# First expert layer's weights in 4 MiB transfers with 32 KiB pieces, in a hybrid mixer and mixture-of-experts block

## The chip, the cores and the metric

The kernel runs on one core of a Trainium2 chip. The metric is the device time of one execution in microseconds, from inputs in HBM to output in HBM. It is written in Bass: each engine (TensorE, here PE; VectorE, DVE; ScalarE, ACT; SyncE, SP) has its own instruction stream, and the streams meet only at semaphores. All large loads are DMAs that SP issues, in the order of its program, onto 16 DMA engines.

## The reference

`x` is 256 tokens of width 1024 in float32. A first part mixes tokens in three branches (an RWKV-7 recurrence, sliding-window attention, attention to a memory), gates and merges them, and adds the result to `x`. The second part is where the change lies: a router picks 4 of 32 experts per token, and each expert is a two-layer network.

```python
logits = (xt @ w_router + b_router)
top_vals, top_idx = lax.top_k(logits, TOP_K)
gates = jax.nn.softmax(top_vals, axis=-1)
...
h = x_pad[tok] @ w1[e] + b1[e]              # w1[e]: 1024 x 2048, 8 MiB
y = clamped_swiglu(h) @ w2[e] + b2[e]       # w2[e]: 1024 x 1024, 4 MiB
...
return rms_norm(h, final_norm_w)
```

The experts' weights are 32 x 12 MiB = 384 MiB, and each is read once.

## The kernel before

**The mixer** runs first. Its weights come in 42 loads (`NMIX`), chunks of at most 1 MiB, in an order that `mixer_chunks` writes out by hand: input projections, memory projections, then for each branch four gate chunks and two branch chunks, and last four chunks of `w_out`.

**The ring.** Weights live in a ring of 16 slots of 1 MiB (`RING`, 8 KiB in each of the 128 partitions). Slots 0 to 5 are narrow ones of their own, at the head of the tensor `ring`. Slots 6 to 15 lie in memory that the mixer uses for other things, at the offsets of `WIDE_AT` (in KiB per partition; offsets below 48 continue the tensor `ring`, the others are in the tensor `upper`). Only the last ten mixer chunks use them, and SP waits before the first load into each region: on `pv_sb`, `y_ps` and `y_rwkv_sb` (lines 366 to 371), which say that what the region held is dead. After the mixer, the experts' weights go round all 16 slots.

**The expert stage.** Each expert takes 12 places of the ring (`CPE`): 8 for the first layer, 4 for the second. `place` turns a running number into a slot. SP's order is: first layer of expert 0, then for each expert r the first layer of r+1 and the second layer of r; at the very end the second layer of the last expert. `load_w1` issues four transfers of 2 MiB per expert, each into two neighbouring slots (`twin_slot`); a partition p gets rows 4p+j and 4p+j+1 of a block of 512 rows, which is 16 KiB in one piece. `load_w2` issues two of 2 MiB, with 16 KiB pieces too, and for the last expert four of 1 MiB.

PE counts each 1 MiB chunk it has used in one semaphore, `slots_used`; before a transfer SP waits until the chunks that were in its slots have been counted. Each transfer announces its landing in `slot_full` of its first slot. PE's order for a pair of experts is in `pair`: `up` of the even expert (first layer, 8 chunks), `down` of the expert before (second layer, 4 chunks), transposes of the activations (`turn`), `up` of the odd expert with the gate transposes and two scatters of the previous pair between its chunks (`between`), `gather` of the next pair's tokens, `down` of the even expert, `turn`. DVE and ACT compute the activation between an `up` and its `turn`. All matrix products go through one helper, so that they carry line 457 in the profile.

After the last pair: `turn_gates`, `down` of the last expert, two scatters, the final norm and the store.

Of the kernel before, what the change touches and what calls it, by code (L numbers as in the profile page):

```python
# [16 lines left out]
P = 128  # L17
D = 1024
T = 256
KC = D // P  # L20
# [10 lines left out]
NCH = T // CH  # L31
# [19 lines left out]
RING = 16  # L51
NARROW = 6
SLOT = 2048
CPE = 12
GROUP = 4
TURNS = GROUP * CPE // RING

WIDE_AT = (88, 96, 72, 80, 0, 8, 16, 24, 32, 40)


PCOLS = {}
# [78 lines left out]
def build(nc, x, mem, w_in, rwkv_w2, rwkv_a2, rwkv_g2, swa_sinks, w_mem_kv, w_gate, w_branch, w_out,  # L140
          ffn_norm_w, w_router, b_router, w_exp1, b_exp1, w_exp2, b_exp2, final_norm_w, params, consts, out):
    order, slots = mixer_chunks()
    NMIX = len(order)
# [7 lines left out]
    with ExitStack() as ctx:  # L151
# [130 lines left out]
        def slot(s):  # L282
            return ring[:, s * SLOT:(s + 1) * SLOT] if s < NARROW else kb(WIDE_AT[s - NARROW], 8)

        def twin_slot(s):
            return ring[:, s * SLOT:(s + 2) * SLOT] if s < NARROW else kb(WIDE_AT[s - NARROW], 16)


        slot_full = [sem(f"slot_full{s}") for s in range(RING)]
        slots_used = sem("slots_used")  # L290
# [56 lines left out]
        def w2_place(i, g, r, final):  # L347
            return place(g, r * CPE + i + (8 if final else 16))

        def rows(w):  # L350
            return w.rearrange("(c p) f -> p c f", p=P)

        @block.sync
        def _(sp):
            for t in range(TT):
                sp.dma_start(xrows[:, t, :], x[0, t * P:(t + 1) * P, :]).then_inc(x_loaded[t], 16)
            sp.dma_start(prm[:], params).then_inc(prm_loaded, 16)
            sp.dma_start(cst[:, 0:2 * P], consts[:, 0:2 * P]).then_inc(ident_loaded, 16)
            w_in_r = rows(w_in[0])
            kv_r = rows(w_mem_kv[0])  # L360
            out_r = rows(w_out[0])
            for n, (name, c) in enumerate(order):
                s = slots[n]
                if previous[n] is not None:
                    sp.wait_ge(slots_used, previous[n] + 1)
                elif s == NARROW:
                    sp.wait_ge(pv_sb, 4)
                elif s == NARROW + 2:
                    sp.wait_ge(y_ps, NCH)
                elif s == NARROW + 6:  # L370
                    sp.wait_ge(y_rwkv_sb, TT)
                wide = slot(s).rearrange("p (c f) -> p c f", c=2)
                if name == "in_rwkv":
                    dst, src = slot(s)[:, 0:C_RWKV], w_in_r[:, c, 0:C_RWKV]
                elif name == "in_rest":
                    dst, src = slot(s)[:, 0:C_REST], w_in_r[:, c, C_RWKV:C_RWKV + C_REST]
                elif name == "mem_kv":
                    dst, src = wide, kv_r[:, 2 * c:2 * c + 2, :]
                elif name == "gate":
                    dst = slot(s).rearrange("p (c f) -> p c f", c=KC)  # L380
                    src = rows(w_gate[0, c[0]])[:, :, c[1] * 256:(c[1] + 1) * 256]
                elif name == "branch":
                    dst = slot(s).rearrange("p (c f) -> p c f", c=4)
                    src = rows(w_branch[0, c[0]])[:, :, c[1] * 512:(c[1] + 1) * 512]
                else:
                    dst, src = wide, out_r[:, 2 * c:2 * c + 2, :]
                sp.dma_start(dst, src).then_inc(slot_full[s], 16)
                if n == 2:
                    sp.dma_start(memrows, mem[0].rearrange("(t p) d -> p t d", p=P)).then_inc(mem_loaded, 16)
                if n == 3:  # L390

                    sp.dma_start(cst[:, 2 * P:], consts[:, 2 * P:]).then_inc(cst_loaded, 16)
                    sp.dma_start(lora[0:64, :], rwkv_w2[0]).then_inc(lora_loaded, 16)
                    sp.dma_start(lora[64:P, :], rwkv_a2[0]).then_inc(lora_loaded, 16)
                    sp.dma_start(gate2, rwkv_g2[0]).then_inc(lora_loaded, 16)
                    sp.dma_start(sinks[:], swa_sinks.to_broadcast([P, 8])).then_inc(sink_loaded, 16)

            sp.dma_start(b2rows[0:NE, :], b_exp2[0]).then_inc(late_loaded, 16)
            for b in range(2):
                sp.dma_start(wrt[:, 4 * b:4 * b + 4, :], w_router[0, b * 512:(b + 1) * 512, :].rearrange("(p c) e -> p c e", c=4)).then_inc(late_loaded, 16)  # L400
            sp.dma_start(brt[:], b_router.to_broadcast([P, NE])).then_inc(late_loaded, 16)

            def load_w1(q, a, r, zero=False):

                g = q * (NE // GROUP) + a
                for c in range(0, KC, 2):
                    s, _, n = w1_place(c, g, r, zero)
                    sp.wait_ge(slots_used, n + (NMIX - RING + 2))
                    b, j = c // 4, c % 4
                    sp.dma_start(twin_slot(s), w_exp1[0, bass.ds(a * GROUP + r, 1), b * 512:(b + 1) * 512, :]  # L410
                                 .rearrange("a (p c) f -> p a c f", c=4)[:, :, j:j + 2, :].rearrange("p a c f -> p (a c f)"))\
                      .then_inc(slot_full[s], 16)

            def load_w2(q, a, r, final=False):
                g = q * (NE // GROUP) + a
                for i in range(0, 4, 1 if final else 2):
                    s, _, n = w2_place(i, g, r, final)
                    sp.wait_ge(slots_used, n + (NMIX - RING + (1 if final else 2)))
                    b, j = i // 2, 2 * (i % 2)
                    src = w_exp2[0, bass.ds(a * GROUP + r, 1), b * 512:(b + 1) * 512, :].rearrange("a (p c) f -> p a c f", c=4)  # L420
                    if final:
                        sp.dma_start(slot(s), src[:, :, j:j + 2, :].rearrange("p a c f -> p (a c f)")).then_inc(slot_full[s], 16)
                    else:
                        sp.dma_start(twin_slot(s), src.rearrange("p a c f -> p (a c f)")).then_inc(slot_full[s], 16)

            def load_group(q, a, count=GROUP):

                for r in range(count):
                    load_w1(q, a, r + 1)
                    load_w2(q, a, r)  # L430

            def load_pass(q, very_first=False):
                load_w1(q, 0, 0, True)
                if very_first:
                    load_group(q, 0)
                with sp.Fori(1 if very_first else 0, NE // GROUP - 1) as a:
                    load_group(q, a)
                load_group(q, NE // GROUP - 1, GROUP - 1)
                load_w2(q, NE // GROUP - 1, GROUP - 1, True)

                for t in range(TT):
                    sp.wait_ge(final_sb, q * TT + t + 1)
                    sp.dma_start(out[0, t * P:(t + 1) * P, :], outrow[:, t, :]).then_inc(stored, 16)

            load_pass(0, True)
            sp.wait_ge(stored, TT * 16)
            sp.wait_ge(route_done, 1)
            most = sp.value_load(cnti[0:1, 0:1], min_val=0, max_val=T)
            with sp.If(most > SLOTS):
                with sp.Fori(1, PASSES) as q:  # L450
                    load_pass(q)
                sp.wait_ge(stored, PASSES * TT * 16)

        @block.tensor
        def _(pe):
# [439 lines left out]
            def up(g, r, E, N, parity, between, zero=False):  # L895

                for c in range(KC):
                    s, times, n = w1_place(c, g, r, zero)
                    if parity == 0 and c % 4 == 0:
                        pe.wait_ge(xg_sb, N * 2 + c // 4 + 1)  # L900
                    if c % 2 == 0:
                        pe.wait_ge(slot_full[s], times * 16 + 16 * uses[s])
                    for z in range(2):
                        for hf in range(2):
                            last = mm(ps[64 * hf:64 * hf + 64, z, :], xg[:, c, parity * SLOTS:(parity + 1) * SLOTS],
                                      slot(s)[:, hf * D + z:(hf + 1) * D:2], c == 0, c == KC - 1)
                    last.then_inc(slots_used, 1)
                    if between:
                        between(c)
                pe.wait_ge(slots_used, n + (NMIX + 1))  # L910
                pe.sem_inc(up_ps, 1)  # L911

            def down(q, g, r, E, final=False):

                pe.wait_ge(actT_sb, E + 1)
                for i in range(4):
                    s, times, n = w2_place(i, g, r, final)
                    if i % 2 == 0:
                        pe.wait_ge(slot_full[s], times * 16 + 16 * uses[s])
                    elif final:  # L920
                        pe.wait_ge(slot_full[s], q * 16 + 16 * (uses[s] + 1))
                    for cc in range(2):
                        k = 2 * i + cc
                        for dh in range(2):
# [821 lines left out]
```

## Time and profile before

| | us |
|---|---|
| median of 3 runs | 1319.02 (1318.52 to 1319.63) |
| the profiled execution | 1318.95 |
| its span, first to last instruction | 1317.1 |
| PE busy | 1221.2 (93%) |
| DVE busy | 349.0 (27%) |
| ACT busy | 199.0 (15%) |
| bytes moved | 449.72 MB, mean 341 GB/s over the span |

The page divides the span in 40 slices of 32.9 us. The mixer takes the first 11 or so, the experts the rest. A busy digit of PE means that matmuls were in its pipe, not that it ran at its peak. Landing time of a DMA counts from its issue, so it contains the wait behind transfers issued before it.

### The profile page before, as it was taken

To read this page: it belongs to the slowest core of one execution; us is meant where nothing else is said; L and a number is where in the kernel's file an instruction comes from. 1 tells how busy PE (TensorE), PEld (TensorE's weight loads), DVE (VectorE), ACT (ScalarE), POOL (GpSimd) and SP (SyncE) were. 2 spreads that over 40 slices of the span, in tenths; PEclk is the share of its full clock that TensorE was granted. 3 is DMA by queue.
4 is the path that set the end of the run, shared out by engine and by line. 5 is a ranking of instruction groups with operands and counts; after the bars stand their busy time and mean duration, and the time that the engine had idled before them with its cause. 6 is when DMAs were issued, how large, how long until landed. Compare 5 with 4: busy or idle time off the path is not lost.

```text
span 1317.1 us, 15444 instructions
## 1 busy us (share of the span) xinstructions
PE 1221.2 (93%) x6534; PEld 599.7 (46%) x6534; DVE 349.0 (27%) x574; ACT 199.0 (15%) x381; POOL 0.2 (0%) x4
## 2 busy tenths in 40 slices
PE   7999989999989999999999889898989989898986
PEld 6886778888553333333323233232323323232322
DVE  2146472211123221231212222121222222121222
ACT  1224522200121110111101011110101011110102
POOL 0000000000000000000000000000000000000000
PEclk9999999999979999999999999999999999999998
DMA  8353201595449999999999999999999999999994
GB/s 340 114 165 131 65 3 34 196 389 197 145 153 399 426 428 426 428 428 429 427 427 428 429 429 428 426 429 429 428 428 428 427 429 428 429 428 428 426 427 197
DMA packets 50799, 449.72 MB, mean 341 GB/s; under 512 B 4512, under 2 KB 17184, under 8 KB 25920
## 3 DMA queue, kind: packets, MB, share of 16 engines
q1 hardware_dynamic: 50272, 447.48, 82.2%
q10 hardware_dynamic: 480, 1.57, 0.4%
q8 instruction: 34, 0.56, 0.2%
q14 instruction: 13, 0.11, 0.0%
HBM read 447.99 MB, written 1.05 MB: 341 GB/s over the span
## 4 chain that ended last, share of the span: by engine, by line
PE 63%; DMA 30%; DVE 4%; ACT 1%; issue 1%; SPq 0%; PEldq 0%; DVEq 0%
PE ps L457 61%; DMA ring<-in_w_exp 30%; DVE ring L1380 0%; PE ps L934 0%; DVE upper L1471 0%; PE ps L692 0%; DMA xrows<-in_x 0%; ACT ring L1134 0%; PE ps L473 0%; ACT factors L1261 0%; DVE upper L1585 0%; PE ps L601 0%; DVE ring L1377 0%; ACT ring L1160 0%; PE ps L842 0%
## 5 line engine op out<-in xcount | busy, mean ns | idle before, releaser
L457 PE MATMUL ps<-ring,upper 128*64 128x512 f32 (+4 forms) x2928 | 572.0, 535 | 40.8 <-DMA ring<-in_w_exp 36.3
L457 PEld LDWEIGHTS ps<-ring,upper 128*64 128x64 f32 (+2 forms) x2928 | 181.6, 137 | 392.0 <-issue 325.6
L457 PE MATMUL ps<-upper 128*64 128x512 f32 (+6 forms) x1624 | 282.3, 441 | 17.0 <-DMA upper<-in_w_exp 8.2
L457 PEld LDWEIGHTS ps<-upper 128*64 128x64 f32 (+3 forms) x1624 | 143.3, 162 | 147.9 <-issue 129.2
L457 PE MATMUL ps<-xT,ring 128*128 128x256 f32 x672 | 150.7, 382 | 0.0
L457 PEld LDWEIGHTS ps<-xT,ring 128*128 128x128 f32 x672 | 127.2, 191 | 18.6 <-issue 1.3
L1668 DVE TENSOR_TENSOR xrows<-xrows,ps 128x1024 f32<-128x1024 f32 x32 | 39.1, 1221 | 314.2 <-PE ps L457 314.2
L1647 DVE TENSOR_TENSOR upper<-ps,merged 128x512 f32<-128x512 f32 x32 | 22.1, 692 | 377.2 <-PEq L911 377.2
L1255 ACT ACTIVATE upper<-upper 128x512 f32<-128x512 f32 x32 | 20.2, 631 | 544.0 <-DVE upper L1650 544.0
L1261 ACT ACTIVATE factors<-ps 64x512 f32<-64x512 f32 x64 | 37.9, 592 | 202.7 <-PEq L929 201.9
L457 PE MATMUL ps<-factors,upper 128*128 128x512 f32 x128 | 63.2, 617 | 1.5 <-ACT factors L1261 1.5
L457 PE MATMUL ps<-upper,ring 128*128 128x256 f32 (+1 forms) x272 | 57.3, 371 | 0.0
L457 PEld LDWEIGHTS ps<-upper,ring 128*128 128x128 f32 (+1 forms) x272 | 45.8, 194 | 8.7 <-issue 2.8
L1640 DVE STREAM_SHUFFLE merged<-merged 128x1024 f32<-128x1024 f32 x32 | 43.2, 1351 | 0.0
L457 PEld LDWEIGHTS ps<-factors,upper 128*128 128x128 f32 x128 | 21.8, 189 | 43.7 <-issue 43.7
L1660 DVE TENSOR_TENSOR upper<-upper 128x512 f32<-128x512 f32 x32 | 34.0, 1063 | 1.2 <-ACT upper L1255 0.2
L934 PEld LDWEIGHTS ps<-cst,upper 128*128 128x128 f32 x128 | 13.5, 141 | 37.1 <-issue 35.2
L934 PE MATMUL ps<-cst,upper 128*128 128x128 f32 x128 | 20.9, 286 | 9.3 <-PE ps L457 8.0
L457 PE MATMUL ps<-ring,merged 128*128 128x512 f32 x64 | 27.8, 592 | 0.0
L1509 DVE TENSOR_TENSOR upper<-upper,ps 128x512 f32<-128x512 f32 x8 | 5.5, 688 | 72.3 <-PE ps L457 72.3
L1251 ACT ACTIVATE upper<-ps 128x512 f32<-128x512 f32 x32 | 17.4, 596 | 34.8 <-PE ps L457 34.8
L1655 DVE SCALAR_TENSOR_TENSOR upper<-upper 128x512 f32<-128x512 f32 x32 | 22.2, 693 | 1.1
(210 smaller groups left out, 477.8 us busy)
## 6 DMA issues: line engine op xcount, KB each, us to landing
ring<-in_w_exp SPq DMA_DIRECT2D x142, 2048.0 KB, 32.5
upper<-in_w_exp SPq DMA_DIRECT2D x48, 2048.0 KB, 33.6
ring<-in_w_gate SPq DMA_DIRECT2D x9, 1024.0 KB, 5.1
ring<-in_w_in SPq DMA_DIRECT2D x8, 896.0 KB, 10.5
ring<-in_w_in SPq DMA_DIRECT2D x8, 640.0 KB, 3.9
ring<-in_w_branch SPq DMA_DIRECT2D x5, 1024.0 KB, 5.1
ring<-in_w_mem_kv SPq DMA_DIRECT2D x4, 1024.0 KB, 4.9
ring<-in_w_out SPq DMA_DIRECT2D x4, 1024.0 KB, 14.4
```

The source lines that it names most:

```text
L457: return pe.matmul(o, l, r, start=start, stop=stop, skip_group_check=True)
L934: last = pe.transpose(ps[:, 2, m * P:(m + 1) * P], act_[:, m * P:(m + 1) * P], ident)
L1251: act.activation(xg[:, 4 * b:4 * b + 4, :], ps[:, 4 + b, :].rearrange("p (c s) -> p c s", c=4), ACT.Copy).then_inc(xg_sb, 1)
L1255: act.activation(sig, glu, ACT.Sigmoid, scale=ALPHA).then_inc(sig_sb, 1)
L1261: act.activation(yrow[64 * parity:64 * parity + 64, dh * 512:(dh + 1) * 512], ps[64 * dh:64 * dh + 64, 3, :], ACT.Copy).then_inc(yrow_sb, 1)
L1509: link(TTn(gsig[:, m % 2, :], gsig[:, m % 2, :], ps[:, 7, :], ALU.mult))
L1640: dve.stream_shuffle(b1all, b1rows, [e] * NE).then_inc(b1_spread, 1)
L1647: TTn(glu, ps[:, 0, :], b1all[:, 0:D:2], ALU.add).then_inc(glu_raw, 1)
L1655: STT(lin, lin, 1.0, glu, ALU.add, ALU.mult).then_inc(prod_sb, 1)
L1660: TTn(act_.rearrange("p (c q) -> p q c", c=4), lin.rearrange("p (q c) -> p q c", c=4), sig.rearrange("p (q c) -> p q c", c=4), ALU.mult).t ...
L1668: TTn(a, a, ps[:, bank:bank + 2, :], ALU.add).then_inc(acc_sb, 1)
```

## The change

First-layer weights are loaded in two transfers of 4 MiB per expert, each a whole block of 512 rows into four slots, with 32 KiB in one piece per partition. SP waits for four released slots instead of two, and PE waits once per four chunks. The order of `WIDE_AT` is sorted so that slots 4 to 7, 8 to 11 and 12 to 15 each lie in one stretch; slots 6 and 7 now sit at offsets 0 and 8, whose first load waits on `y_ps`, and slots 8 to 15 follow `y_rwkv_sb`. Second-layer transfers stay at 2 MiB (1 MiB for the last expert); since a 4 MiB transfer announces itself in the semaphore of its first slot only, the second half of a second layer gets a semaphore of its own choosing (`w2_full`).

```diff
-WIDE_AT = (88, 96, 72, 80, 0, 8, 16, 24, 32, 40)
+WIDE_AT = (0, 8, 16, 24, 32, 40, 72, 80, 88, 96)
...
-        def twin_slot(s):
-            return ring[:, s * SLOT:(s + 2) * SLOT] if s < NARROW else kb(WIDE_AT[s - NARROW], 16)
+        def joined(s, n):
+
+            if s < NARROW:
+                return ring[:, s * SLOT:(s + n) * SLOT]
+            return kb(WIDE_AT[s - NARROW], 8 * n)
...
+        def w2_full(s, i, r):
+
+            return slot_full[(s, 9, 2 * (r % GROUP) + 1, 11)[i]]
...
                 elif s == NARROW:
-                    sp.wait_ge(pv_sb, 4)
+                    sp.wait_ge(y_ps, NCH)
                 elif s == NARROW + 2:
-                    sp.wait_ge(y_ps, NCH)
-                elif s == NARROW + 6:
                     sp.wait_ge(y_rwkv_sb, TT)
...
-                for c in range(0, KC, 2):
+                for c in (0, 4):
                     s, _, n = w1_place(c, g, r, zero)
-                    sp.wait_ge(slots_used, n + (NMIX - RING + 2))
-                    b, j = c // 4, c % 4
-                    sp.dma_start(twin_slot(s), w_exp1[0, bass.ds(a * GROUP + r, 1), b * 512:(b + 1) * 512, :]
-                                 .rearrange("a (p c) f -> p a c f", c=4)[:, :, j:j + 2, :].rearrange("p a c f -> p (a c f)"))\
-                      .then_inc(slot_full[s], 16)
+                    sp.wait_ge(slots_used, n + (NMIX - RING + 4))
+                    sp.dma_start(joined(s, 4), w_exp1[0, bass.ds(a * GROUP + r, 1), c * P:(c + 4) * P, :]
+                                 .rearrange("a (p c) f -> p (a c f)", c=4)).then_inc(slot_full[s], 16)
...
-                    if c % 2 == 0:
+                    if c % 4 == 0:
                         pe.wait_ge(slot_full[s], times * 16 + 16 * uses[s])
...
-                    if i % 2 == 0:
-                        pe.wait_ge(slot_full[s], times * 16 + 16 * uses[s])
+                    if i == 0:
+                        pe.wait_ge(w2_full(s, 0, r), times * 16 + 16 * uses[s])
+                    elif i == 2:
+                        pe.wait_ge(w2_full(s, 2, r), g * 16 + 16 * (uses[2 * (r % GROUP) + 1] + (r >= 0)))
```

## Rows read from the trace of the kernel before

**Rows 1.** The page: rate of the DMA engines in 40 equal slices of the span.

```profile
GB/s 340 114 165 131 65 3 34 196 389 197 145 153 399 426 428 426 428 428 429 427 427 428 429 429 428 426 429 429 428 428 428 427 429 428 429 428 428 426 427 197
```

**Rows 2.** DMA over 460 to 1160 us: packets, bytes, rate.

```profile
DMA packets 20580, 299.75 MB, mean 428 GB/s; under 512 B 2284, under 2 KB 2284, under 8 KB 2284
```

**Rows 3.** Chain that ended last, by time: start, us, what.

```profile
461.25 16.90 PE ps L457 x64
...
515.12 16.90 PE ps L457 x64
```

**Rows 4.** PE timeline, 1137 to 1152: start, duration, operation, [idle before <- releaser].

```profile
1137.37 3.65 PE L457 MATMUL ps<-ring,upper 128*64 128x512 f32 x16 [1.16 <-DMA ring<-in_w_exp]
1142.17 3.65 PE L457 MATMUL ps<-ring,upper 128*64 128x512 f32 x16 [1.15 <-DMA ring<-in_w_exp]
...
1147.07 2.02 PE L457 MATMUL ps<-ring,upper 128*64 128x512 f32 x8 [0.30 <-DMA ring<-in_w_exp]
...
1151.96 2.02 PE L457 MATMUL ps<-ring,upper 128*64 128x512 f32 x8 [0.55 <-DMA ring<-in_w_exp]
```

**Rows 5.** Windows: busy per engine, clock, DMA share and GB/s last.

```profile
280.00:286.00 6.00, 6.00 (x29) 5.28 (x29) 0.00 (x0) 0.60 (x1) 0.00 (x0) 1.00 1.03 411
262.00:270.00 8.00, 8.00 (x39) 7.04 (x38) 1.38 (x2) 0.60 (x1) 0.00 (x0) 1.00 1.08 361
```

**Rows 6.** SP timeline, 366 to 436: issues of expert weights.

```profile
366.57 0.33 SPq L410 DMA_DIRECT2D ring<-in_w_exp  x1
390.74 0.33 SPq L424 DMA_DIRECT2D ring<-in_w_exp  x1
...
401.54 0.33 SPq L410 DMA_DIRECT2D upper<-in_w_exp  x1
411.60 0.33 SPq L410 DMA_DIRECT2D upper<-in_w_exp  x1
417.26 0.33 SPq L410 DMA_DIRECT2D ring<-in_w_exp  x1
...
424.46 0.33 SPq L424 DMA_DIRECT2D ring<-in_w_exp  x1
...
435.45 0.33 SPq L410 DMA_DIRECT2D ring<-in_w_exp  x1
```

**Rows 7.** Windows of 2 us at the start of the stream.

```profile
390.00:392.00 2.00, 2.00 (x12) 0.67 (x10) 0.00 (x0) 0.00 (x0) 0.00 (x0) 1.00 0.62 115
392.00:394.00 2.00, 2.00 (x12) 0.57 (x10) 0.00 (x0) 0.00 (x0) 0.00 (x0) 1.00 0.59 205
...
412.00:414.00 2.00, 2.00 (x10) 0.61 (x5) 0.00 (x0) 0.00 (x0) 0.00 (x0) 1.00 0.81 213
...
418.00:420.00 2.00, 2.00 (x12) 0.65 (x10) 0.00 (x0) 0.00 (x0) 0.00 (x0) 1.00 0.86 262
```

**Rows 8.** Timelines of DVE and SP around 250: end of the recurrence, first wide load.

```profile
245.38 0.69 DVE L1541 TENSOR_TENSOR upper<-upper,ring 128x512 f32<-128x512 f32 x1
...
256.05 1.13 SPq L387 DMA_DIRECT2D upper<-in_w_gate  x2
```

**Rows 9.** PE timeline: the gather between two experts.

```profile
424.58 3.81 PE L457 MATMUL ps<-upper 128*128 128x128 f32 x32 [0.16 <-PE ps L457]
```

**Rows 10.** PE timeline, 1265 to 1303: the last expert.

```profile
1265.59 2.02 PE L457 MATMUL ps<-ring,upper 128*64 128x512 f32 x8 [0.55 <-DMA ring<-in_w_exp]
...
1270.39 2.02 PE L457 MATMUL ps<-ring,upper 128*64 128x512 f32 x8 [0.46 <-DMA ring<-in_w_exp]
...
1281.72 3.82 PE L457 MATMUL ps<-upper 128*64 128x512 f32 x16
...
1290.21 3.65 PE L457 MATMUL ps<-ring,upper 128*64 128x512 f32 x16 [0.70 <-DMA ring<-in_w_exp]
...
1295.88 7.09 PE L457 MATMUL ps<-ring,upper 128*64 128x512 f32 x32 [1.02 <-ACT upper L1266]
```

**Rows 11.** DVE timeline: the last expert's activation ends.

```profile
1288.40 1.06 DVE L1660 TENSOR_TENSOR upper<-upper 128x512 f32<-128x512 f32 x1
```

More of the change, by code:

```diff
@@ L421, in load_w2 @@
                     if final:
-                        sp.dma_start(slot(s), src[:, :, j:j + 2, :].rearrange("p a c f -> p (a c f)")).then_inc(slot_full[s], 16)
-                    else:
-                        sp.dma_start(twin_slot(s), src.rearrange("p a c f -> p (a c f)")).then_inc(slot_full[s], 16)
+                        src = src[:, :, j:j + 2, :]
+                    sp.dma_start(joined(s, 1 if final else 2), src.rearrange("p a c f -> p (a c f)")).then_inc(w2_full(s, i, r), 16)
             def load_group(q, a, count=GROUP):
@@ L917, in down @@
                     s, times, n = w2_place(i, g, r, final)
-                    if i % 2 == 0:
-                        pe.wait_ge(slot_full[s], times * 16 + 16 * uses[s])
+                    if i == 0:
+                        pe.wait_ge(w2_full(s, 0, r), times * 16 + 16 * uses[s])
+                    elif i == 2:
+                        pe.wait_ge(w2_full(s, 2, r), g * 16 + 16 * (uses[2 * (r % GROUP) + 1] + (r >= 0)))
                     elif final:
-                        pe.wait_ge(slot_full[s], q * 16 + 16 * (uses[s] + 1))
+                        pe.wait_ge(w2_full(s, i, r), q * 16 + 16 * (uses[8 + i] + 1))
                     for cc in range(2):
```

## The prediction

> **What bounds the kernel now.** I read the page's bandwidth strip first. From slice 13 of 40 on it stands at 426 to 429 GB/s until the last slice [rows 1]; over 460 to 1160 us the mean is 428 GB/s [rows 2], or 428.2 from its 299.75 MB in 700 us. So the 16 DMA engines never rest in the expert stage, although PE looks 93% busy. The chain of waits seems to say otherwise: it lies mostly on PE. But a step on it that begins with a slot released by PE and ends with a landing contains the wait behind all transfers queued before it, so I price both sides instead. Two experts are 24 MiB, 25.17 MB, which take 58.8 us at 428.2 GB/s. The same pair costs PE 53.9 us (the start of the same step at 461.25 and 515.12) [rows 3]. DMA is slower by 4.9 us a pair, and later in the trace PE waits for each landing: starts at 1137.37, 1142.17, 1147.07 and 1151.96, each "<-DMA", 4.8 to 4.9 us apart, which is one 2 MiB transfer [rows 4]. The end of the kernel is therefore: the moment from which the stream is unbroken, plus the bytes left over the rate, plus a tail behind the last landings. Whatever the change does must show in one of these three.
>
> **The change part by part.** *The rate.* Of the 384 MiB of expert weights the first 16 MiB fill the ring early; of the stream behind it, experts 2 to 31, the first layer has 30 x 2 = 60 joined transfers of 4 MiB, each 2 x 4.898 = 9.80 us today, 588 us together. Today's pieces are 16 KiB: 299.75 MB in 20580 packets, of which 2284 are tiny, 16 for each of 143 transfers (the completion marks) [rows 2]. The change halves the number of both, pieces and marks, in the first layer. What is that worth? No row has 32 KiB pieces, so I extrapolate. At 280 to 286 us the engines move w_out in 4 KiB pieces at 411 GB/s [rows 5]: 4096 x 16 / 411 = 159.5 ns for a piece on one engine. The 16 KiB piece takes 16384 x 16 / 428.2 = 612.2 ns. The slope is 0.0368 ns per byte and what stays fixed is 8.6 ns. A 32 KiB piece would take 1215.8 ns in place of 1224.4: 0.70%, 4.1 us of 588. The 262 to 270 stretch (1 and 2 KiB pieces, 361 GB/s [rows 5]; read as 1 KiB) gives 7.6 ns and 3.6 us. I take 4.0 us gained. The near bound is nothing, if the fixed part goes with bytes or a piece is cut in two again; the far one I set at double, 8 us, since the two stretches are mixed and short.
>
> The Trainium skill, "DMA: Bandwidth & Descriptors", section "Anatomy of one DMA", fits a DMA as about 2.0 us plus bytes at 436 GB/s. Taken as time in the stream, that would give 6.8 us for 2 MiB and save 2 us in each of 60 merges; the landings 4.8 to 4.9 us apart [rows 4] contradict it, so here the 2 us overlap with the next transfer. Its slope alone leaves 0.085 us per transfer, and an estimate of 5.1 us for 60 marks fewer, near my own value.
>
> *The start of the stream.* The ring is full and DMA idle until PE consumes the first expert. SP issues at 390.74; the 2 us windows from 390 carry 115 and 205 GB/s, together 1.5 us' worth at full rate by 394, so data flow as from 392.5, 1.76 us after the issue [rows 6, 7]. Four 2 MiB transfers end at 412.1. The next was released and issued at 411.60, so flows from 413.4: 1.3 us gap; it ends 418.3, the next, issued 417.26, flows from 419.0: 0.8 us gap; the windows 412:414 (213 GB/s) and 418:420 (262 GB/s) show just these holes [rows 6, 7]. After that each transfer is issued before the one ahead of it ends. Sum 2.1 us.
> With the change, the two second-layer transfers go as before and end at 402.3. The joined transfer of slots 4 to 7 needs all four released, which is the 401.54 event: flow from 403.3, gap 1.0. It ends 413.1. The joined one of slots 8 to 11 needs the 417.26 event: flow from 419.0, gap 5.9. It ends 428.8, the two second-layer ones behind it (the later issued at 424.46) end 438.6, and slots 0 to 3 are free at 435.45 [rows 6], 437.2 with the latency: no gap, nor later, since PE then releases faster than DMA fills. Sum 6.9 us, so **4.8 us lost**. PE does not meet these gaps itself: the third expert's weights land by about 415 and 431, and PE reaches them after 435.45. But each microsecond that the engines rest is paid at the end, because the stream is unbroken from there.
> The reordered WIDE_AT and its waits cost nothing. The wide slots now wait for y_ps and y_rwkv_sb instead of pv_sb and y_ps, but SP reaches these transfers only at 256.05, held by the narrow slots, and the step that completes y_rwkv_sb starts at 245.38 and takes 0.69 [rows 8]: 10 us of cover. If that cover were gone, gate and branch loads for branch 0 would follow at once. The last quarter of the ring is now one transfer issued with the release at 366.57 [rows 6] instead of two; it lands near 380 and PE wants it only after 411.
>
> *The middle.* In each expert PE now gets its first layer in two lumps 9.8 us apart. I walk one pair, with the first lump landing at 0: even expert, 7.3 us of matmuls (3.65 for two chunks [rows 4]), second lump at 9.8 to 17.1, second layer landed 14.7 and 19.6, done 24.4, transposes to 25.1. Odd expert: lump at 29.4, four chunks with gate transposes and one scatter to 39.3, the rest and a scatter to 48.6, gather 3.8 [rows 9] to 52.5, second layer and transposes to 60.5. The next lump landed at 58.8, so PE is 1.7 us late, and again on time within the following even expert, where it idles. A slot is released at most some 11 us after landing; its next use is 12 MiB, 29 us, behind. SP's waits for four slots hold up only the second-layer transfers queued behind them, and with three quarters of the ring in flight no engine notices. Cost nothing. PE also executes two fewer waits per expert: nothing.
>
> *The tail.* Today the last second-layer pair of transfers and four single ones follow the last first-layer ones. PE starts the last expert's first layer at 1265.59, ends its eight chunks with two scatters at 1285.5 (1281.72 + 3.82), and then waits until 1290.21 for the last 2 MiB of the previous second layer; the last down starts at 1295.88, 5.67 later [rows 10]. The landings are L = 1290.2 for that transfer, L - 9.8 = 1280.4 for the last of the first layer, 1270.4 (the wait at 1270.39 [rows 10]) for its middle. With joined transfers PE can start only at 1270.6, not 1265.59. Four chunks, transposes and a scatter are 9.9 us (4 x 1.85, 0.4, 1.9, and seams): 1280.5, as the second lump lands. The other four and a scatter, 9.45, end at 1289.95. Then second layer, 0.3 + 3.65 to 1293.9, and its second half, landed long before, from there: its start moves from 1290.21 to 1293.9 and with it the last down from 1295.88 to 1299.6. **3.7 us lost.** The activation is no later bound: it ends 4 us after the first layer (1285.5 against 1288.40 + 1.06 [rows 10, 11]), 1293.9, and the last weights land at 1300.0 while down needs them at 1305. All this shifts with the stream.
>
> Sum: 4.8 + 3.7 - 4.0 = +4.5 us. The profiled execution took 1318.95 us with a span of 1317.1; the median of the runs is 1319.02, the same. Forecast **1323.5 us**.
>
> **The rivals.**
> *No gain in rate:* 428.2 GB/s is what the ports or the memory give, and pieces of 32 KiB travel no better than 16 KiB, or are cut back. For it: 4 times the piece from 4 to 16 KiB brought only 4%, and part of that may be the mixed content. Against it: fixed costs at 1 and 4 KiB agree (7.6 and 8.6 ns). Time 1318.95 + 8.5 = 1327.5.
> *The ceiling is reached:* the overhead is larger than I extrapolate, and joined transfers run nearly without any. The gain has to be over 5.9 us, 1.0% of 588, to bring the result within the limit of measurement. It would need more than twice the fixed part of each transfer that I extrapolate to vanish, but the extrapolation rests on two short stretches. At 1.6%, 9.4 us, the time is 1318.1. The Trainium skill, same page, section "Where 436 GB/s comes from", has 435.2 GB/s as the fabric's ceiling; 428.2 to 435.2 is that 1.6%.
> *Faster, by the order of reading:* today a first-layer transfer takes every other 16 KiB of HBM, half of each 32 KiB row group, while the second layer's blocks are whole. If this skipping cost, the joined ones, whole 4 MiB blocks, would win it back; the place is the 588 us of first-layer streaming, the price each percent 5.9 us, and it decides for faster from 1.9% (8.5 + 2.6 us). At 3% the time is 1318.95 + 8.5 - 17.6 = 1309.9. Against it: first-layer landings are 4.90, 4.89 and 4.80 us apart [rows 4, 10], a second-layer one 4.80 [rows 4]. If skipping cost 3%, first-layer ones would be 0.15 us longer each time.
> *Start or tail not paid:* if PE's releases at 401 to 417 come earlier, or the tail's wait is elsewhere, 3 to 4 us vanish: about 1320.
>
> **How the numbers follow.** Forecast, with its gain between 2 and 5.8 us: 0.50. No gain: 0.20. Ceiling: 0.10. Order of reading: 0.09. A loss not paid: 0.11. Measurement can tell 0.2%, 2.6 us, from no change. Slower: 0.48 of the forecast and 0.20 of no gain, 0.68. Same: 0.09 of the ceiling, 0.11 of a loss not paid and 0.02 at the forecast's edge, 0.22. Faster: the order of reading and 0.01 of the ceiling, 0.10. The range must leave out at most 2 in 10: from 1318.8, which takes in most of the cases of small loss, to 1328.5, which is no gain at all and 1 us for the hand-made walk.
>
> **What would show it.** The strip should read 430 or more in place of 428 in the same stretch, and in 700 us some 6,900 of the 20,580 packets should be gone (half of two thirds). The windows of 2 us from 402 and from 412 to 420 should show about 1 and 6 us of rest. The last down should start 5.7 us after the previous second layer's second half without a DMA wait between. A rate still at 428 means the second case; over 435 the fourth. The prediction is wrong if the middle shows any window under 425 GB/s, that is if lumps of four slots starve the queue.

## The result and the profile after

The changed kernel took 1324.21 us (median of 6 runs, 1321.79 to 1324.76) against 1319.33 of the kernel before, measured beside it: a ratio of 1.0032 with a 95% interval of 1.0022 to 1.0043. Measured once more in another set, beside 1319.81, it took 1323.9 us, ratio 1.0025 (1.0016 to 1.0034). It is slower by 4 to 5 us; 1323.5 was forecast. The profiled execution is the fastest of the first six, 1321.79 us with a span of 1319.9. So a second profile, near the median (1324.26 us, span 1322.4), is read beside it below; half of the difference between the two turned out to have a cause.

The strip of the changed kernel answers to [rows 1]. The beginning of the stream is the 13th figure, 342 where it was 399. After it, up to the last slice, the figures go from 425 to 433, 18 of the 26 at 430 or more, where 426 to 429 stood before:

```profile
GB/s 343 110 167 128 65 3 40 199 391 145 159 194 342 432 428 431 432 431 430 432 426 429 431 433 430 432 432 432 425 430 433 432 429 430 431 430 428 429 428 154
```

Over 460 to 1160 us there are 13780 packets instead of 20580, and 301.35 MB instead of 299.75 [rows 2]. That is 0.53% more in the same time, or 0.8% on the first layer alone, which is two thirds of the bytes. Six thousand eight hundred packets are gone, close to the 6,900 of the count of halved pieces and marks:

```profile
DMA packets 13780, 301.35 MB, mean 430 GB/s; under 512 B 1529, under 2 KB 1529, under 8 KB 1529
```

The issues of SP at the start of the stream answer to [rows 6]:

```profile
401.23 0.33 SPq L414 DMA_DIRECT2D ring<-in_w_exp  x1
...
416.93 0.33 SPq L414 DMA_DIRECT2D ring<-in_w_exp  x1
```

and the windows of 2 us to [rows 7] (last two columns: share of the 16 engines busy, GB/s):

```profile
402.00:404.00 2.00, 1.81 (x4) 0.66 (x4) 1.97 (x5) 1.97 (x3) 0.00 (x0) 1.00 0.98 270
412.00:414.00 2.00, 2.00 (x9) 0.66 (x6) 0.00 (x0) 0.00 (x0) 0.00 (x0) 1.00 0.12 49
414.00:416.00 2.00, 2.00 (x9) 0.59 (x9) 1.03 (x1) 0.00 (x0) 0.00 (x0) 1.00 0.00 0
416.00:418.00 2.00, 2.00 (x10) 0.57 (x8) 0.20 (x1) 0.00 (x0) 0.00 (x0) 1.00 0.30 82
418.00:420.00 2.00, 2.00 (x12) 0.68 (x10) 0.00 (x0) 0.00 (x0) 0.00 (x0) 1.00 0.95 328
```

Both holes are where they were expected. Read as time at 428 GB/s, the first is 0.7 us and the second 5.9 us (379, 428, 346 and 100 GB/s missing, over 2 us each). Bytes are a surer measure than windows of 2 us, in which a few pieces more or less count for much. Up to 450 us the kernel before had moved 86.13 MB and the changed one 84.52 (84.52 in its second profile too): 1.61 MB less, which is 3.8 us at 428 GB/s. That is what the start costs.

The tail, PE's timeline in the first profile (start, duration, operation, [idle before <- what ended it]), answers to [rows 10]:

```profile
1260.27 7.09 PE L459 MATMUL ps<-upper 128*64 128x512 f32 x32 [0.32 <-PE ps L459]
...
1270.09 2.02 PE L459 MATMUL ps<-ring,upper 128*64 128x512 f32 x8 [1.95 <-DMA ring<-in_w_exp]
...
1289.68 7.09 PE L459 MATMUL ps<-ring,upper 128*64 128x512 f32 x32 [0.32 <-PE ps L459]
...
1298.78 7.09 PE L459 MATMUL ps<-upper 128*64 128x512 f32 x32 [1.02 <-ACT upper L1270]
```

and in the second profile:

```profile
1271.12 3.33 PE L459 MATMUL ps<-ring,upper 128*64 128x512 f32 x8 [3.16 <-DMA ring<-in_w_exp]
...
1292.00 7.09 PE L459 MATMUL ps<-ring,upper 128*64 128x512 f32 x32 [0.31 <-PE ps L459]
...
1301.10 7.09 PE L459 MATMUL ps<-upper 128*64 128x512 f32 x32 [1.02 <-ACT upper L1270]
```

In the first profile PE's wait for the last expert's first layer ends at nearly the same moment as the wait at its middle did before (1270.09 against 1270.39), in the second 0.7 us later than before (1271.12): the lost start and the gained rate nearly cancel. From there to the last down it took 25.49 us before, 28.69 in the first profile and 29.98 in the second, and behind the down all three are alike (21.1 to 21.3 us to the end of the span). The second profile has a low clock in its tail. Its first chunk takes 3.33 us in place of 2.02, and the windows (clock granted in the third column from the end, 1.00 being 2.4 GHz) say why:

```profile
1268.00:1271.00 3.00, 0.00 (x0) 0.00 (x0) 0.00 (x0) 1.11 (x2) 0.00 (x0) 0.92 1.01 437
1271.00:1275.00 4.00, 3.88 (x12) 1.24 (x14) 0.00 (x0) 0.15 (x1) 0.00 (x0) 0.63 0.99 426
```

In 1271 to 1275 the mean clock is 0.63, so PE spent most of the stretch at the lower of its two levels, 1.2 GHz, having waited 3.16 us before. The 2.5 us between the two profiles are thus 1.3 us of slow first instructions and 1.0 us of a later landing (1271.12 against 1270.09); why the landing is later stays open.

The length of the wait alone does not tell whether the clock falls. The first profile has 1.95 us and then 2.02 us for eight instructions, at a clock of 1.00; the second has, at 860.09 us, a wait of 1.94 us and then 2.98 us for eight, with a mean clock of 0.61 over 860 to 864. The wait says that the clock can fall, not that it will.

### The profile page after: what moved, and what is told of

It reads as the page before. It is cut to its first block, busy times and chain, and to the rows that moved or that the text cites. A ratio compares the mean times of both kernels' runs of the same rounds, so it can differ in the third digit from the quotient of the medians.

```text
span 1319.9 us, 15236 instructions
## 1 busy us (share of the span) xinstructions
PE 1231.4 (93%) x6534; PEld 606.9 (46%) x6534; DVE 349.2 (26%) x574; ACT 199.0 (15%) x381; POOL 0.2 (0%) x4
## 4 chain that ended last, share of the span: by engine, by line
PE 67%; DMA 26%; DVE 4%; ACT 1%; issue 1%; SPq 0%; PEldq 0%; DVEq 0%
PE ps L459 65%; DMA ring<-in_w_exp 26%; PE ps L949 1%; DVE ring L1384 0%; DVE upper L1475 0%; PE ps L694 0%; DMA xrows<-in_x 0%; ACT ring L1138 0%; PE ps L938 0%; PE ps L475 0%; ACT factors L1265 0%; DVE upper L1589 0%; PE ps L844 0%; PE ps L603 0%; DVE ring L1381 0%
## 5 line engine op out<-in xcount | busy, mean ns | idle before, releaser
L459 PE MATMUL ps<-ring,upper 128*64 128x512 f32 (+4 forms) x2928 | 583.8, 546 | 38.2 <-DMA ring<-in_w_exp 34.0
L459 PE MATMUL ps<-upper 128*64 128x512 f32 (+5 forms) x1592 | 270.3, 440 | 12.2 <-PE ps L459 6.5
L459 PE MATMUL ps<-xT,ring 128*128 128x256 f32 x768 | 171.6, 381 | 0.0
L459 PEld LDWEIGHTS ps<-xT,ring 128*128 128x128 f32 x768 | 145.1, 190 | 21.0 <-issue 1.3
L459 PE MATMUL ps<-upper,ring 128*128 128x256 f32 (+1 forms) x304 | 64.2, 370 | 0.0
L459 PEld LDWEIGHTS ps<-upper,ring 128*128 128x128 f32 (+1 forms) x304 | 51.8, 193 | 9.6 <-issue 3.0
L938 PE MATMUL ps<-cst,upper 128*128 128x128 f32 x128 | 21.2, 289 | 9.3 <-PE ps L459 7.6
L459 PE MATMUL ps<-upper,merged 128*128 128x512 f32 x64 | 27.8, 592 | 0.0
```

The lines of the kernel that those rows point to most:

```text
L459: return pe.matmul(o, l, r, start=start, stop=stop, skip_group_check=True)
L938: last = pe.transpose(ps[:, 2, m * P:(m + 1) * P], act_[:, m * P:(m + 1) * P], ident)
```

## The experiments

All times are medians beside runs of the kernel before on the same chip; the differences are worked out against those: 1319.85 for the first four experiments, 1319.69 for the whole blocks, the three experts and the busy PE, 1319.81 for the four kernels between (the changed kernel again, the start, the tail and both ends).

### Release in lumps of four, nothing else

```diff
-                    sp.wait_ge(slots_used, n + (NMIX - RING + 2))
+                    if c % 4 == 0:
+                        sp.wait_ge(slots_used, n + (NMIX - RING + 4))
```

> The kernel before (16 KiB pieces, 2 MiB transfers, PE waits per 2 MiB, old WIDE_AT), but SP waits for four released slots before it issues the two first-layer transfers of a block. It has the start term alone. Theory of three terms: the engines rest 1 us near 402 and 5 to 6 us between 412 and 419, the rate stays 428, the last down starts 5.7 us after the last wait: 1319.3 + 4.8 = 1324.1 us. Rival, rest at the start is not paid at the end (PE catches up): 1319.3 us. Rival, lumps of four slots starve the queue all along: a rate under 425 and more than 1330 us.

Measured: 1325.22 us, +5.4; ratio 1.0043 (1.0030 to 1.0056). The rate over 460 to 1160 is 428 GB/s, and the second hole is that of the changed kernel, with 16 KiB pieces and old `WIDE_AT`:

```profile
412.00:414.00 2.00, 2.00 (x9) 0.66 (x6) 0.00 (x0) 0.00 (x0) 0.00 (x0) 1.00 0.08 33
414.00:416.00 2.00, 2.00 (x8) 0.49 (x9) 1.12 (x1) 0.00 (x0) 0.00 (x0) 1.00 0.00 0
416.00:418.00 2.00, 2.00 (x12) 0.57 (x10) 0.10 (x1) 0.00 (x0) 0.00 (x0) 1.00 0.40 82
```

Rest of the engines at 412 to 419 us is paid at the end. That PE never misses these data while they are late does not help. But not all of the 5.4 us is that rest. The last down of this profile starts here (1295.88 before):

```profile
1299.87 7.09 PE L458 MATMUL ps<-ring,upper 128*64 128x512 f32 x32 [1.02 <-ACT upper L1267]
```

That is 4.0 us later, and by 450 us 84.51 MB had been moved against 86.13, 3.8 us' worth. The other 2.3 us of this profile's span (1323.4 against 1317.1) lie behind the last down: 23.5 us to the end against 21.2. No row ties them to the start of the stream, and their cause stays open.

### Use in lumps of four, nothing else

```diff
-                    if c % 2 == 0:
+                    if c % 4 == 0:
                         pe.wait_ge(slot_full[s], times * 16 + 16 * uses[s])
+                        pe.wait_ge(slot_full[s + 2], times * 16 + 16 * uses[s + 2])
```

> The kernel before, but PE waits for both landings of a block before the first of its four chunks. It has the coarse consumption alone: releases come later in the middle, the tail is that of the change. Theory of three terms: no rest of the DMA engines beyond before's 2 us, since at the start the data lie there long before; rate 428; the last down starts 3 to 3.7 us later: 1319.3 + 3.5 = 1322.8 us. Rival, the clock: PE's longer waits (2.65 us in the changed kernel, with a granted clock of 0.97) slow its first matmuls behind each wait and the tail too: 1 to 3 us more, 1324 to 1326 us. Rival, the tail is not on the path: 1319.3 us.

Measured: 1324.9 us, +5.1; ratio 1.0038 (1.0025 to 1.0051), where the tail alone was to give 3.5. The rival with the clock is nearer. In its profile the last expert starts like this:

```profile
1272.91 2.86 PE L457 MATMUL ps<-ring,upper 128*64 128x512 f32 x8 [2.66 <-DMA ring<-in_w_exp]
...
1303.15 7.09 PE L457 MATMUL ps<-ring,upper 128*64 128x512 f32 x32 [1.02 <-ACT upper L1267]
```

From the landing to the last down it is 30.24 us, 4.75 more than before: 3.2 of coarse use and 1.5 of slow matmuls. This profiled execution is the longest of its five (1326.34 us), and its landings were 2.5 us late already; of that its first 60 us explain 0.6 (390 GB/s against 394), the rest stays open.

### Four-MiB transfers with 16 KiB pieces

```diff
-                    sp.dma_start(joined(s, 4), w_exp1[0, bass.ds(a * GROUP + r, 1), c * P:(c + 4) * P, :]
-                                 .rearrange("a (p c) f -> p (a c f)", c=4)).then_inc(slot_full[s], 16)
+                    j = c // 2
+                    sp.dma_start(joined(s, 4).rearrange("p (b f) -> p b f", b=2),
+                                 w_exp1[0, bass.ds(a * GROUP + r, 1), :, :]
+                                 .rearrange("a (b p c) f -> p (a b) c f", c=4, b=2)[:, :, j:j + 2, :].rearrange("p b c f -> p b (c f)")).then_inc(slot_full[s], 16)
...
-                            last = mm(ps[64 * hf:64 * hf + 64, z, :], xg[:, c, parity * SLOTS:(parity + 1) * SLOTS],
+                            last = mm(ps[64 * hf:64 * hf + 64, z, :], xg[:, (0, 1, 4, 5, 2, 3, 6, 7)[c], parity * SLOTS:(parity + 1) * SLOTS],
```

> The changed kernel with its 4 MiB transfers, but each transfer takes two pieces of 16 KiB per partition (rows of both halves of the first layer; PE takes the chunks in the order 0, 1, 4, 5, 2, 3, 6, 7). Number of transfers and of completion marks as in the changed kernel, number of pieces as before. If the rate comes from the piece: 428 GB/s in the stream and 1324.2 + 4.6 = 1328.8 us. If it comes from fewer transfers and marks: 430.5 GB/s and 1324.2 us. If from the order of reading (whole blocks): 428 GB/s, like the piece; the next kernel tells these two apart.

Measured: 1328.18 us, +8.3; ratio 1.0068 (1.0054 to 1.0082). The gain is gone and both losses are left (DMA over 460 to 1160 us):

```profile
DMA packets 19817, 299.76 MB, mean 428 GB/s; under 512 B 1520, under 2 KB 1520, under 8 KB 1520
```

A third fewer completion marks (1520 against 2284) move no more bytes than before, 299.76 MB against 299.75. The transfer's size alone is worth nothing here. What the change brought hangs on the longer piece, or on the reading of whole blocks, which this kernel gave up as well.

### Two-MiB transfers with 32 KiB pieces

```diff
-                    sp.dma_start(joined(s, 4), w_exp1[0, bass.ds(a * GROUP + r, 1), c * P:(c + 4) * P, :]
-                                 .rearrange("a (p c) f -> p (a c f)", c=4)).then_inc(slot_full[s], 16)
+                    src = w_exp1[0, bass.ds(a * GROUP + r, 1), c * P:(c + 4) * P, :].rearrange("a (p c) f -> p (a c f)", c=4)
+                    sp.dma_start(joined(s, 4)[0:64, :], src[0:64, :]).then_inc(slot_full[s], 16)
+                    sp.dma_start(joined(s, 4)[64:P, :], src[64:P, :]).then_inc(slot_full[2 + 8 * (r % 2) + c], 16)
```

> The changed kernel with each 4 MiB block loaded by two transfers of 2 MiB, 64 partitions each, 32 KiB in one piece per partition; PE waits for both. Number of pieces as in the changed kernel, number of transfers and marks as before. If the rate comes from the piece: 430 to 430.5 GB/s and 1324.2 us. If it comes from fewer transfers: 428 GB/s and 1328.8 us. A third outcome: 64 partitions do not spread over the 16 engines as 128 do, the rate falls well under 428 and the time rises by tens of us.

Measured: 2172.52 us, ratio 1.64, the third outcome. The experiment says nothing of the piece, but it shows what half the partitions cost (one window of its trace):

```profile
800.00:900.00 100.00, 51.20 (x194) 17.62 (x192) 8.56 (x13) 5.66 (x10) 0.00 (x0) 0.76 1.00 228
```

The DMA share is 1.00, all 16 engines are occupied, and yet they carry 228 GB/s, second-layer transfers with all 128 partitions included. Of the 40 slices of 2.5 us in this window 35 read 190 to 236 GB/s; two short stretches reach 341 to 393.

### Whole blocks with 16 KiB pieces

The kernel before with one part of the change alone. (The matching layout of the tokens and of the router's weights is left out of the lines below.) The question was still open whether the long piece brings the rate or the reading of HBM in order.

```diff
-                    sp.dma_start(twin_slot(s), w_exp1[0, bass.ds(a * GROUP + r, 1), b * 512:(b + 1) * 512, :]
-                                 .rearrange("a (p c) f -> p a c f", c=4)[:, :, j:j + 2, :].rearrange("p a c f -> p (a c f)"))\
+                    sp.dma_start(twin_slot(s), w_exp1[0, bass.ds(a * GROUP + r, 1), c * P:(c + 2) * P, :]
+                                 .rearrange("a (p c) f -> p (a c f)", c=2))\
```

> The kernel before, but each first-layer transfer of 2 MiB reads one whole block of 256 rows from HBM (partition p gets rows 2p and 2p+1, 16 KiB in one piece) instead of every other 16 KiB of a block of 512 rows; the normalized tokens and the router's weights are laid out to match, which cuts two VectorE instructions ahead of the router into four. Transfers, pieces, releases and waits are as before. If the changed kernel's rate comes from the longer piece: 428.2 GB/s here and 1319.6 us. If it comes from reading whole blocks in order: 430.5 GB/s and 1319.6 - 4.5 = 1315.1 us.

Measured: 1319.65 us against 1319.69; ratio 0.9998 (0.9988 to 1.0007), 299.87 MB over 460 to 1160. The order of reading alone is worth nothing. Together with the third experiment the length of the piece remains, by elimination: no run at full rate has the long piece alone, and 4 MiB in whole blocks with 16 KiB pieces was not run, so an effect of size and order together is not excluded.

### One expert at the start in 2 MiB

```diff
+                    if halves is not None:
+                        src = w_exp1[0, bass.ds(a * GROUP + r, 1), c * P:(c + 4) * P, :].rearrange("a (p c) f -> p a c f", c=4)
+                        for j in (0, 2):
+                            sp.wait_ge(slots_used, n + (NMIX - RING + 2 + j))
+                            sp.dma_start(joined(s, 4)[:, j * SLOT:(j + 2) * SLOT], src[:, :, j:j + 2, :].rearrange("p a c f -> p (a c f)"))\
+                              .then_inc(slot_full[halves + c if j else s], 16)
+                        continue
...
-                    load_group(q, 0)
+                    load_group(q, 0, cut=2, halves=2)
```

Here and in the experiments below that cut further experts, PE's wait for the second landing of each block is left out of the lines shown.

The control in this set is the changed kernel itself:

> The changed kernel once more, as the base for the three that follow and to see the tail in a second profile. In its first profile the last expert's first wait was 1.95 us and the clock stayed at 1.00 behind it; behind waits of 2.46 us and more it read about 0.6 for some 4 us. Theory: in most executions the last wait is over 2.4 us, the first lump then takes 1.2 to 1.6 us more, which is the part of the loss that the first profile (1321.8 us, the lowest of its six executions) lacks: 1324 us, and in a profile at that time the last expert starts at a low clock. Rival: the 2.4 us between that profile and the median lie in the mixer or the rate: same clock of 1.00 behind the last wait.

Measured 1323.9 us, with the second profile shown above: the last wait 3.16 us, then the low clock, as expected. The clock explains 1.3 of the 2.5 us between the profiles, not all of them, and that most executions have it is not shown by one profile.

> The changed kernel, but the first layer of the third expert alone (the two transfers before which the DMA engines rested 1 and 6 us) in 2 MiB transfers with 16 KiB pieces, as before. Theory of three terms: the rest at 412 to 419 us shrinks to before's 2 us, the end comes 4.8 us less 0.15 for the lost pieces earlier: 1324.2 - 4.7 = 1319.5 us. Rival, the stall is not paid at the end: 1324.2 us.

Measured: 1323.02 us, +3.2; ratio 1.0020 (1.0011 to 1.0029), 0.9 us below the changed kernel instead of 4.7. The expectation missed. The windows show that the rest did go from 412 to 419, and where it went to:

```profile
412.00:414.00 2.00, 2.00 (x9) 0.57 (x6) 0.00 (x0) 0.00 (x0) 0.00 (x0) 1.00 0.60 139
418.00:420.00 2.00, 2.00 (x12) 0.61 (x10) 0.00 (x0) 0.00 (x0) 0.00 (x0) 1.00 0.94 270
...
434.00:436.00 2.00, 1.84 (x11) 0.42 (x8) 0.00 (x0) 0.05 (x1) 0.00 (x0) 1.00 0.02 8
436.00:438.00 2.00, 2.00 (x12) 0.90 (x14) 0.00 (x0) 1.73 (x3) 0.00 (x0) 1.00 0.93 262
```

SP issues the fourth expert's first transfer when PE has released slots 0 to 3:

```profile
435.85 0.33 SPq L421 DMA_DIRECT2D ring<-in_w_exp  x1
```

In the changed kernel the two transfers ahead of it were still under way then, because they themselves had been held up. Once they are not, it is its turn to come late. Over 390 to 450 us the rate is 374 GB/s against 367 of the changed kernel, worth 1.0 us, and 0.9 us is what the median gained. The size of the moved rest differs between profiles: with both ends cut, further down, the same release comes at 434.33 and the rate over this stretch is 385, where PE's granted clock is 0.97 in place of 0.94.

### The last expert in 2 MiB, and both ends

```diff
-                load_group(q, NE // GROUP - 1, GROUP - 1)
+                load_group(q, NE // GROUP - 1, GROUP - 1, cut=3, halves=10)
```

> The changed kernel, but the first layer of the last expert alone in 2 MiB transfers. Theory of three terms: the last down starts 3.5 us earlier against the landings, and the last wait of PE is short, so that the clock stays: 1324.2 - 3.5 - 1.5 + 0.15 = 1319.4 us. Rival, no clock term in the tail: 1320.9 us. Rival, the tail is bound by the last second-layer landings: 1324.2 us.

Measured: 1320.15 us, +0.3; ratio 0.9998 (0.9989 to 1.0007), 3.75 us below the changed kernel. The last expert no longer waits at its start, so neither the late start nor the clock are left:

```profile
1260.17 7.09 PE L466 MATMUL ps<-upper 128*64 128x512 f32 x32 [0.32 <-PE ps L466]
...
1267.97 2.02 PE L466 MATMUL ps<-ring,upper 128*64 128x512 f32 x8
...
1296.67 7.09 PE L466 MATMUL ps<-upper 128*64 128x512 f32 x32 [1.02 <-ACT upper L1280]
```

From its start to the last down it is 28.70 us, all of it PE's work. It could not start at 1265.6, as before, because the lumps ahead of it had kept PE: the second layer before it only ends at 1267.3. The last down comes 0.8 us later than before (1296.67 against 1295.88), and what it hangs on is now PE, not a landing.

> The changed kernel with both: third and last expert's first layers in 2 MiB transfers, all between in 4 MiB with 32 KiB pieces. If the terms add up, only the gain in rate is left against the kernel before: 1319.6 - 4.3 = 1315.3 us, faster than both kernels, rate in the stream 430.5 GB/s. Rival, the long pieces' gain is lost again in PE's stretches at the low clock: 1319 us.

Measured: 1317.47 us, -2.3; ratio 0.9986 (0.9977 to 0.9995). Faster than both kernels, by half of what was expected. Some 1.2 us of the other half is the rest that had moved (85.60 MB by 450 us against 86.13 before).

### Three experts in 2 MiB

```diff
-                load_group(q, 0, cut=2, halves=2)
+                load_group(q, 0, cut={2: 2, 3: 10})
```

> The changed kernel with the first layers of the third, fourth and last experts in 2 MiB transfers. The profile with the third alone in 2 MiB showed the rest moved rather than gone: at 434 us the engines stood for 3 us, because the next joined transfer (slots 0 to 3) was released only at 435.8 and now nothing was left in the queue before it. Theory: with the fourth expert cut as well no rest but before's 2 us is left; against both ends cut (1317.5) 3 us earlier, 1314.7 us. Rival, the remaining rest is not what holds the end: 1317.5 us.

Measured: 1315.81 us (1313.8 to 1316.82), -3.9; ratio 0.9964 (0.9951 to 0.9978). Over 390 to 450 us, where the kernel before moved 394 GB/s and the changed one 367, it moves 397:

```profile
390.00:450.00 60.00, 57.63 (x260) 20.37 (x257) 13.58 (x22) 6.38 (x10) 0.00 (x0) 0.97 0.98 397
```

The expectation was 1314.7, its rival 1317.5; the time is between them and nearer to the first. At the start nothing is lost any more, and this is the fastest of all kernels here. The tail still loses something:

```profile
1263.91 2.02 PE L466 MATMUL ps<-ring,upper 128*64 128x512 f32 x8
...
1292.60 7.09 PE L466 MATMUL ps<-upper 128*64 128x512 f32 x32 [1.02 <-ACT upper L1280]
```

By 1270 us this kernel has moved 439.13 MB, the kernel before 437.23: 4.4 us' worth at 428 GB/s. Its last down is only 3.3 us earlier (1292.60 against 1295.88). PE starts the last expert without a wait and works 28.69 us up to the last down, so the end is now held by PE, which the lumps ahead have made late.

### PE kept busy before the wait

```diff
+                if parity == 1 and keep_busy:
+                    for _ in range(4):
+                        mm(ps[0:64, 0, :], xg[:, 0, SLOTS:2 * SLOTS], hn[:, 0, 0:512])
```

> The changed kernel with added work: from the third pair on PE runs four more matmuls of 128x512 (about 1.8 us, results overwritten) between the end of its previous work and the wait for the odd expert's first landing. If the low clock behind that wait costs 1.2 to 1.6 us in the tail: the clock stays at 1.00 there, the mean granted clock is back at 0.985 or more, and the time is 1324.0 - 1.3 = 1322.7 us; executions under 1322 are the rule rather than the exception. If the clock costs nothing at the end: 1324.0 us. If the added matmuls delay the landing's use: over 1325 us.

Measured: 1322.3 us (1321.51 to 1323.26), +2.6; ratio 1.0018 (1.0009 to 1.0027). The mean granted clock over the kernel is 0.989 in place of 0.973, and the last expert starts at full speed after more than 3 us of added work:

```profile
1266.37 3.65 PE L459 MATMUL ps<-upper 128*64 128x512 f32 x8
1270.26 2.02 PE L459 MATMUL ps<-ring,upper 128*64 128x512 f32 x8 [0.25 <-DMA ring<-in_w_exp]
...
1298.94 7.09 PE L459 MATMUL ps<-upper 128*64 128x512 f32 x32 [1.02 <-ACT upper L1273]
```

The four calls took 3.65 us, twice what was reckoned, and still ended before the landing. The stretch is 28.68 us, like the profile without the low clock. The medians agree with 1.3 us gained (+2.6 us here, +4.1 for the changed kernel beside its own base in another set), though the intervals of the two kernels overlap, so the gain itself is not shown. That executions under 1322 us would be the rule did not come true: 2 of 11 are. That the added work does not lengthen the kernel, and that the clock stays, is shown.

## Why the prediction held, point by point

*What bounds the kernel*: right. Nearly all that moved the time did so through the unbroken stream's beginning, its rate, or the tail (the 2.3 us behind the last down in the first experiment are the exception, and unexplained); the low clock and the lumpy waits of the middle cost nothing, since the changed kernel moves 429 to 432 GB/s in every 100 us from 500 to 1200.

*The rate*: forecast 4.0 us, in fact some 4.4 (0.53% of the 830 us from 450 to 1280). The fixed part of a piece, extrapolated to 8.6 and 7.6 ns from shorter pieces, comes out near 9.8 ns (0.8% of the 1224.4 ns that two short pieces take), an estimate that takes the whole gain for a fixed part of the piece. The text lumped pieces and completion marks together. A third fewer marks brought nothing; by elimination it is the piece. "No gain" fell with the 301.35 MB, "faster, by the order of reading" with the fifth experiment, "start or tail not paid" with the first two. "The ceiling is reached" fell with 0.8% measured on the first layer where it needed 1.0%. It was made to look dearer than it was: 1.0% is 12.2 ns, 1.4 times the fixed part that was extrapolated; only its 1.6% is more than twice.

The Trainium skill, "DMA: Bandwidth & Descriptors", section "Anatomy of one DMA", gives its fit for DMAs issued by GpSimd; SP issues the ones here. The prediction used its slope for an estimate of 5.1 us from fewer marks (5.3 by the division: 4.898 less 4.81 us, 60 times). The size was near, the reason was not: a third fewer marks moved the same 299.76 MB.

*The start*: the mechanism was right, the size 3.8 us instead of 4.8. The holes in the windows give 6.6 us against about 2.0 before, 4.6, but the bytes by 450 us give 3.8, in both profiles of the changed kernel and in the kernel with this term alone, whose last down came 4.0 us late. The median of that kernel lost 5.4 (4.0 to 7.4 by its interval), of which its profile has 2.3 us behind the last down. The sentence that "later" there was no gap was right for this kernel and for a reason that it did not give: the queue had been filled up by the earlier stall. It was read as spare time and was not, which is why the expectation for the start alone missed by 3.5 us.

*The tail*: the mechanism was right, its size 3.2 us instead of 3.7 (28.69 less 25.49 us). The walk had put the last expert's start at the landing and was right there, and no wait for a DMA stands between it and the last down, as forecast; it took 29.0 us from the one to the other (1270.6 to 1299.6) where 28.69 were measured. It missed a second term: the wait of PE before the last expert becomes longer, and behind such a wait the clock can fall. That is worth 1.3 us in the second profile and about 1.5 in the experiment on PE's waits.

*The sum*: +4.5 us was forecast, +4.9 and +4.1 us were measured in the two sets. That it came this close is in part luck. The three terms as measured are 3.8 + 3.2 - 4.4 = 2.6 us, which fits the first profile (2.8 us more span than before); they were 1.9 us under the forecast's, and what made up for it in the second profile are two things that the forecast did not have, 1.3 us of low clock and a landing some 1 us later. The direction and the three places are shown by the experiments; that the sum fell within half a microsecond is not.

*The middle*: forecast at nothing, and so it was, but PE's waits there are not harmless in kind. The walk through one pair has PE wait up to some microseconds for the odd expert's first lump, and this is what one of them looks like in the changed kernel:

```profile
1152.15 3.18 PE L459 MATMUL ps<-ring,upper 128*64 128x512 f32 x8 [2.65 <-DMA ring<-in_w_exp]
```

Eight instructions take 3.18 us instead of 2.02. With DMA as the bound there is time for it. The prediction named any window under 425 GB/s as the sign of a starved queue. One 33 us slice of the second profile's strip does read 423, but the engines' share is 0.99 over 1157 to 1190, so nothing starved there: the sign was set too tight for windows of that length. *The reordered ring* cost nothing, as forecast: SP reaches the first wide slot at 255.68 (256.05 before).

## What to carry to other kernels

In a stage bound by DMA, price a change of granularity at three places first: where the stream begins (a larger unit waits for more buffers when the ring is full and the queue empty), its rate, and the work behind the last landings. Then look whether the compute engine, held up by larger lumps, comes to hold the end itself, as PE did here once the other losses were cured. A gap that seems harmless because the queue is full at that moment may only be hidden by an earlier stall; removing the first one shows the second. Use large pieces in the middle of a stream and small transfers at its two ends: here that turned 0.3% slower into 0.4% faster.

## What the runs showed of the hardware

- A 32 KiB piece per partition moves 0.8% faster than two of 16 KiB (430.5 against 428.2 GB/s with two thirds of the bytes in long pieces). Neither a transfer twice the size (428.2) nor whole blocks in order (299.87 MB against 299.75) does this by itself; that it is the piece is by elimination.
- Transfers to 64 partitions at a time kept all 16 engines at a share of 1.00 and moved 228 GB/s. The Trainium skill's "SBUF — State Buffer", section "Door 1: The DMA port swizzle", has partitions 0 to 63 reach only 8 of the 16 ports and gives 196 GB/s for a 1 MiB transfer to them. By that rule the loss has its reason in the ports, and the trace agrees in size: 35 of the 40 slices of 2.5 us between 800 and 900 us read 190 to 236 GB/s. Why two transfers to opposite halves together do no better was not tried by itself.
- PE's granted clock fell from 1.00 to a mean of 0.63 over 4 us behind a wait of 3.16 us, and the same instructions behind the same wait ran at full speed (2.02 us) where it was 1.95 us. Elsewhere in the second profile a wait of 1.94 us was enough (2.98 us for eight instructions, clock 0.61), so no length of wait can be read from these rows as the limit. "TensorE: Matmul & The Clock Gate" of the Trainium skill has the section "Part 1: The HAM clock gate", by which the array falls to 1.2 GHz when it has been idle; the kernel kept busy by worthless matmuls stayed at 0.989, as that would have it.
